# Second attention of a decoder trunk: heads in pairs of column halves, output projection placed between the head steps

## The chip, the cores and the metric

One core of a Trainium2 chip runs the kernel. The metric is the device time of one execution in microseconds (us), as the median of several runs. TensorE (PE, its weight loads PEld), VectorE (DVE), ScalarE (ACT), GpSimd (POOL) and SyncE (SP, which issues the weight DMAs) each work through their own list of instructions in program order and wait for each other by semaphores.

## The reference

Two layers of a decoder on a batch of 256 tokens, width 1024, all in float32. Layer 0 is sparse attention and a dense SwiGLU. Layer 1, where the change lies, is multi-head latent attention and then a top-2-of-8 expert SwiGLU:

```python
def mla_mixer(h, ...):                      # h: (1, 256, 1024), 16 heads
    cq, ckv, k_pe = _split(h @ w_in, [384, 256, 32])
    q = (rmsnorm(cq, q_a_norm) @ w_uq).reshape(B, S, 16, 96)
    kv = (rmsnorm(ckv, kv_a_norm) @ w_ukv).reshape(B, S, 16, 128)
    k_nope, v = kv[..., :64], kv[..., 64:]
    ...                                     # k_pe joined to every head, QK-norm, rotary on 32 columns
    o = causal_attention_blocks(q, k, v)    # softmax(q k^T / sqrt(96), causal) v
    return o.reshape(B, S, 1024) @ w_out    # w_out: 1024 x 1024
x = x + mla_mixer(rmsnorm(x)); h = rmsnorm(x)
y = sum over e of combine[:, e] * swiglu(h, w_gate[e], w_up[e], w_down[e])   # 8 experts, inner width 3584
```

## The kernel before, in words

**Products.** A large product is made of three matmuls in a rounded format: the data and the weight are each split into a high and a low part, and high x high, low x high and high x low are added in PSUM. The weights come from memory in chunks of at most 128 x 2048 floats, numbered in the order in which they are used (`C_LAT`, `C_HEADS`, `C_OUTO`, `C_ROUTE`, `C_MOE` are the first chunks of the latent projection, the head projections, the output projection, the router and the experts). ACT makes the high part of a chunk, DVE the low part (`split`, lines 487 and 954). `split_to(c)` in the list of ACT or DVE says how far this must have come at that place. A chunk's high slot and raw slot are used again when a later chunk comes round, which is counted by `mm_done`, the number of chunks that PE has finished.

**Group stage.** The 16 heads are projected in four groups of four (chunks `C_HEADS` to `C_HEADS`+7). For each group ACT squares, DVE normalises and rotates (lines 1330 to 1370), PE transposes each head (`turn_group`, line 2001) and ACT copies the transposed heads to `qkT` (`group_evac`, line 748).

**Head stage.** `heads(NH, NH, ...)` stands in the lists of PE, ACT, DVE and POOL and runs over the 16 heads one by one. For each head: PE makes the logits (lines 1797, 1798) in PSUM bank 4 or 5; DVE adds the mask and takes the row maximum (1061, 1071) into one of four buffers `lg1[h % 4]`; ACT takes exponentials and row sums (559, 561); DVE takes the reciprocal (1075) and scales the first 128 columns (1077), POOL scales the other 256 (1664); PE transposes the result (1807) into bank 6 or 7, ACT copies it to `pT1` (554); PE multiplies by V (1815, 1816) into half of the rows of bank 0 or 1; after every second head ACT makes the high part `a_hi` (566) and DVE the low part `a_lo` (1082, semaphore `at_olo`). The heads overlap: PE's list has, for step s, the logits of head s, the transposes of head s-3 and the V product of head s-4.

**Output projection.** After `at_olo` has reached 16 (all pairs of heads), PE multiplies by the four chunks of `w_out` (lines 1696, 1697, 1700), adds nothing in between but one set of transposes, and the router follows (`route`, line 2042, in two halves, each after a residual on DVE, line 1227, and transposes, line 1742). SP loads the first expert chunks: four when raw slots come free, then it waits for `at_olo` = 16 and issues chunks 4, 5, 13, 14, 15, then 6 to 11 as slots come free, and from chunk 16 on it needs the experts' order (semaphore `order_set`), which is made from the router's output.

The first attention of the same kernel (layer 0) already runs in pairs: `pair_step`, `pair_mix`, `head_turn` (lines 1749 to 1788) on PE with `pair_logits`, `pair_norm`, `pair_low` on DVE.

## Time and profile before

| | us |
|---|---|
| median of 3 runs (lowest, highest) | 1339.3 (1339.26, 1339.61) |
| the profiled execution | 1338.47 |
| its span | 1336.3 |
| PE, DVE, ACT, POOL busy | 1276.0, 749.7, 633.7, 39.0 |
| head stage, 417.4 to 451.2 us of the span | 33.8 |
| output projection, 451.2 to 474.1 us | 22.9 |
| experts, from 492.4 us to the end | 844 |

The span is the stretch from the first to the last instruction of the profiled execution. "Busy" of PE counts matmuls whose ends are modelled and overlap, so the distance between two starts is the better measure of what one costs. Groups of rows from the trace stand further below; all their times are microseconds from the start of the span.

### The profile page before, as it was taken

How to read it: one execution, taken by the hardware profiler on the slowest of the kernel's cores; microseconds unless marked ns; L12 is line 12 of the kernel's file. 1: busy time of each engine (PE TensorE's matmuls, PEld its weight loads, DVE VectorE, ACT ScalarE, POOL GpSimd, SP SyncE). 2: the span in 40 equal slices, each digit the busy share in tenths (PEclk: the TensorE clock that was granted, in tenths of full speed). 3: DMA queues.
4: the chain of work that ended last, by engine and by line, in shares of the span. 5: the costliest groups of instructions: out<-in, count | busy, mean ns of one | idle time of the engine just before them, and what ended most of it. 6: DMA issues, size and time to landing. Idle time of an engine off the chain costs nothing.

```text
span 1336.3 us, 15885 instructions
## 1 busy us (share of the span) xinstructions
PE 1276.0 (95%) x6208; PEld 899.4 (67%) x6209; DVE 749.7 (56%) x933; ACT 633.7 (47%) x730; POOL 39.0 (3%) x48
## 2 busy tenths in 40 slices
PE   7987999999987989999999999999999999999997
PEld 6765788888875778475847565766656675838572
DVE  5876465444487458464727464736646543837370
ACT  5575562434358537263626353625444533626350
POOL 1012000000002200000000000000000000000000
PEclk9998999999998979999999999999999999999999
DMA  9632455364353458799999999999999999999996
GB/s 341 222 127 65 155 189 189 116 228 149 103 165 136 189 213 318 305 390 411 421 421 421 421 417 417 421 421 420 421 418 417 420 421 420 421 418 418 420 421 251
DMA packets 88757, 422.92 MB, mean 316 GB/s; under 512 B 8561, under 2 KB 15463, under 8 KB 57959
## 3 DMA queue, kind: packets, MB, share of 16 engines
q1 hardware_dynamic: 87468, 419.10, 79.5%
q0 software_dynamic: 992, 2.69, 0.6%
q8 instruction: 50, 0.82, 0.2%
q14 instruction: 29, 0.23, 0.0%
q10 hardware_dynamic: 218, 0.08, 0.0%
HBM read 420.77 MB, written 1.07 MB: 316 GB/s over the span
## 4 chain that ended last, share of the span: by engine, by line
PE 84%; DVE 7%; DMA 4%; ACT 3%; issue 2%; SPq 0%; DVEq 0%; ACTq 0%
PE PS L2151 12%; PE PS L2127 11%; PE PS L2131 11%; PE PS L2128 11%; PE PS L2143 7%; PE PS L1696 7%; PE PS L1700 7%; PE PS L1697 7%; DMA raw<-in_w_down_o_dram 3%; DVE w_r L954 2%; PE PS L2158 1%; PE PS L2067 1%; PE PS L2076 1%; ACT w_r L487 1%; PE PS L1815 1%
## 5 line engine op out<-in xcount | busy, mean ns | idle before, releaser
L1377 DVE TENSOR_TENSOR w_r<-raw,w_r 128x2048 fp32r<-128x2048 f32 (+1 forms) x150 | 314.8, 2102 | 179.3 <-ACT w_r L784 178.8
L784 ACT ACTIVATE w_r<-raw 128x2048 fp32r<-128x2048 f32 (+1 forms) x150 | 264.9, 1766 | 205.9 <-PE PS L2131 118.6
L2127 PE MATMUL PS<-w_r,a_hi 128*128 128x512 f32 x512 | 201.8, 394 | 0.0
L2128 PE MATMUL PS<-w_r,a_lo 128*128 128x512 f32 x512 | 199.9, 390 | 0.0
L2151 PE MATMUL PS<-raw,xs 128*64 128x512 f32 (+1 forms) x856 | 169.9, 543 | 0.0
L954 DVE TENSOR_TENSOR w_r<-raw,w_r 128x2048 fp32r<-128x2048 f32 (+4 forms) x69 | 139.3, 2044 | 40.2 <-ACT w_r L487 40.0
L1696 PE MATMUL PS<-w_r,a_hi 128*128 128x512 f32 (+4 forms) x384 | 144.4, 380 | 6.0 <-DVE a_lo L983 5.1
L1697 PE MATMUL PS<-w_r,a_lo 128*128 128x512 f32 (+4 forms) x384 | 141.9, 373 | 0.0
L487 ACT ACTIVATE w_r<-raw 128x2048 fp32r<-128x2048 f32 (+4 forms) x69 | 115.2, 1719 | 15.4 <-PE PS L1700 12.6
L2151 PEld LDWEIGHTS PS<-raw,xs 128*64 128x64 f32 x856 | 58.8, 137 | 92.8 <-issue 84.2
L2127 PEld LDWEIGHTS PS<-w_r,a_hi 128*128 128x128 f32 x512 | 96.2, 188 | 28.0 <-issue 8.5
L2131 PE MATMUL PS<-w_r,a_hi 128*128 128x512 f32 x411 | 112.3, 390 | 0.9 <-DVE w_r L1377 0.9
L2128 PEld LDWEIGHTS PS<-w_r,a_lo 128*128 128x128 f32 x512 | 96.2, 188 | 19.8
L1700 PE MATMUL PS<-w_r,a_hi 128*128 128x512 f32 (+4 forms) x384 | 97.7, 374 | 0.3 <-DVE w_r L954 0.3
L1377 DVE TENSOR_TENSOR slots_r<-slots,w_r 128x2048 fp32r<-128x2048 f32 (+1 forms) x30 | 62.8, 2095 | 57.9 <-ACT w_r L784 57.8
L2131 PEld LDWEIGHTS PS<-w_r,a_hi 128*128 128x128 f32 x411 | 77.0, 188 | 17.8 <-DVE w_r L1377 1.8
L1696 PEld LDWEIGHTS PS<-w_r,a_hi 128*128 128x128 f32 x384 | 72.8, 189 | 20.6 <-issue 7.7
L2143 PE MATMUL PS<-raw,es 128*64 128x512 f32 x376 | 83.1, 593 | 0.0
L1697 PEld LDWEIGHTS PS<-w_r,a_lo 128*128 128x128 f32 x384 | 72.9, 190 | 11.3
L1700 PEld LDWEIGHTS PS<-w_r,a_hi 128*128 128x128 f32 x384 | 69.5, 190 | 13.5 <-DVE w_r L954 1.7
L784 ACT ACTIVATE w_r<-slots 128x2048 fp32r<-128x2048 f32 (+1 forms) x30 | 53.0, 1767 | 48.1 <-DMA slots<-in_w_gate_o_dram 23.8
L2127 PE MATMUL PS<-w_r,e_hi 128*128 128x512 f32 x160 | 64.1, 400 | 1.7 <-ACT w_r L784 1.7
(318 smaller groups left out, 1445.9 us busy)
## 6 DMA issues: line engine op xcount, KB each, us to landing
raw<-in_w_down_o_dram SPq DMA_DIRECT2D x94, 1024.0 KB, 18.8
raw<-in_w_gate_o_dram SPq DMA_DIRECT2D x53, 1024.0 KB, 14.6
raw<-in_w_up_o_dram SPq DMA_DIRECT2D x51, 1024.0 KB, 15.1
raw<-in_w_gate_o_dram SPq DMA_DIRECT2D x53, 768.0 KB, 12.1
raw<-in_w_up_o_dram SPq DMA_DIRECT2D x53, 768.0 KB, 11.7
slots<-in_w_down_o_dram SPq DMA_DIRECT2D x18, 1024.0 KB, 18.3
raw<-in_w_in_e_dram SPq DMA_DIRECT2D x12, 1024.0 KB, 10.5
raw<-in_w_down_e_dram SPq DMA_DIRECT2D x11, 1024.0 KB, 4.8
```

The source lines that it names most:

```text
L487: nc.scalar.activation(w_r[:, hi_slot(c), 0:n], raw[:, c % RAW, 0:n], ACT.Copy).then_inc(hi_done, 1)
L784: nc.scalar.activation(w_r[:, high_slot(g), 0:w], place_of(n)[:, 0:w], ACT.Copy).then_inc(hi_done, 1)
L954: nc.vector.tensor_tensor(w_r[:, c % RAW, 0:n], raw[:, c % RAW, 0:n], w_r[:, hi_slot(c), 0:n], ALU.subtract).then_inc(lo_done, 1)
L1377: nc.vector.tensor_tensor(place_r(n)[:, 0:w], place_of(n)[:, 0:w], w_r[:, high_slot(g), 0:w], ALU.subtract).then_inc(lo_done, 1)
L1696: nc.tensor.matmul(dst, xh, wh, start=first, stop=False)
L1697: nc.tensor.matmul(dst, xl, wh, start=False, stop=False)
L1700: return nc.tensor.matmul(dst, xh, wl, start=False, stop=last)
L2127: nc.tensor.matmul(PS[:, bank, :], xh(x), hi[:, c0:c0 + NT], start=first, stop=False)
L2128: nc.tensor.matmul(PS[:, bank, :], xl(x), hi[:, c0:c0 + NT], start=False, stop=False)
L2131: ins = nc.tensor.matmul(PS[:, bank, :], xh(x), lo[:, c0:c0 + NT], start=False, stop=last)
L2143: ins = nc.tensor.matmul(PS[HALF * h:HALF * h + HALF, SMALL_DOWN, :], es[:, f, :], w[:, kk * D + h * NT:kk * D + (h + 1) * NT], start=f == ...
L2151: ins = nc.tensor.matmul(PS[HALF * h:HALF * h + HALF, bank + b, 0:n], xs[:, at, :], w[:, c0:c0 + n], start=at == 0, stop=at == DC - 1)
```

## The change

Heads of the second attention go in pairs, with the semaphores and functions of the first attention: a step s has the logits of pair s, the transposes of pair s-2 and the V product of pair s-3. All transposes use bank 6, all V products bank 7, where the two heads of a pair use the two column halves of the array. The matmuls of the output projection are cut into 16 pieces (`out_piece(n, dc)`: column half n, rows of 128 inputs dc, six matmuls each) that stand in PE's list between the logits and the second transposes of a step. Steps 0 and 1 stand inside the end of the group stage. On ACT and DVE the splits of chunks stand earlier or elsewhere, and the last pair's result stands behind the first expert chunk's split. SP has chunks 4, 5, 6 before its wait for `at_olo`, and POOL does four heads before it issues one DMA.

```diff
-        lg1, z1 = place(z0, "lg1", [P, 4, LOG])
+        lg1, z1 = place(z0 + 2 * TT * GH * ROPE, "lg1", [P, 4, LOG])
...
# SP
+            sp.wait_ge(sem("at_qk"), 2 * NH)
+            for n in (4, 5):
+                expert_chunk(0, n, 0)
+            ring_chunk(6)
             sp.wait_ge(sem("at_olo"), NH)
-            for n in (4, 5, 13, 14, 15):
+            for n in (13, 14, 15):
                 expert_chunk(0, n, 0)
-            for n in range(6, 12):
+            for n in range(7, 12):
                 ring_chunk(n)
# ACT (heads() is removed)
+            def late_step(s):
+                if s >= 3:
+                    pair_out(s, NH)               # a_hi of pair s-3 from bank 7
+                for r in range(2):
+                    if 2 <= s < NH // 2 + 2:
+                        probs_turned(NH + 2 * s - 4 + r)   # waits at_tr; copy to pT1
+                    if s < NH // 2:
+                        head_exp(NH + 2 * s + r)  # waits at_max
...
-                split_to(C_HEADS + 2 * g + 4)
+                if g == 0:
+                    split_to(C_HEADS + 6)
+                elif g == 1:
+                    split_to(C_HEADS + 7)
+                elif g == 2:
+                    split_to(C_OUTO + 1)
                 if g >= 1:
                     group_evac(g - 1, 0)
-                split_to(C_HEADS + 2 * g + 5)
+                if g < 2:
+                    split_to(C_HEADS + 7 + g)
             group_evac(GROUPS - 2, 1)
+            late_step(0)
             group_evac(GROUPS - 1, 0)
+            late_step(1)
             group_evac(GROUPS - 1, 1)
-            heads(NH, NH, lg1, pT1)
-            spare_root(3)
+            split_to(C_OUTO + 2)
+            late_step(2)
+            late_step(3)
+            split_to(C_OUTO + 3)
+            late_step(4)
+            split_to(C_OUTO + 4)
+            for s in range(5, NH // 2 + 2):
+                late_step(s)
             split_to(C_MOE)
             esplit(0)
+            late_step(NH // 2 + 2)
+            spare_root(3)
             esplit(1)
# DVE, in the last group, before its reciprocal
+                if g == GROUPS - 1:
+                    pair_logits(0, NH)
...
-                split_to(C_HEADS + 2 * g + 4)
+                if g < 3:
+                    split_to(C_HEADS + 6 + g)
...
-                split_to(C_HEADS + 2 * g + 5)
-            heads(NH, NH, lg1, False)
+                if g == 2:
+                    split_to(C_OUTO + 1)
+            pair_logits(1, NH)
+            pair_norm(0, NH)
+            split_to(C_OUTO + 2)
+            pair_logits(2, NH)
+            pair_norm(1, NH)
+            pair_logits(3, NH)
+            pair_norm(2, NH)
+            pair_low(0, NH)
+            split_to(C_OUTO + 3)
+            pair_logits(4, NH)
+            pair_norm(3, NH)
+            pair_low(1, NH)
+            split_to(C_OUTO + 4)
+            for s in range(5, NH // 2):
+                pair_logits(s, NH)
+                pair_norm(s - 1, NH)
+                pair_low(s - 3, NH)
+            pair_norm(NH // 2 - 1, NH)
+            pair_low(NH // 2 - 3, NH)
+            split_to(C_MOE)
+            pair_low(NH // 2 - 2, NH)
-            split_to(C_MOE)
             esplit(0)
+            pair_low(NH // 2 - 1, NH)
             dve.wait_ge(mm_done, C_OUTO + 2)
             residual(0, PS[:, 0:2, :])
# POOL
+            heads(NH, 4, lg1)
             pool.wait_ge(sem("grp_tr"), NH)
             pool.dma_start(ffg[:, :], ffn_norm_o.to_broadcast([P, D])).then_inc(sem("ffg_in"), 16)
-            heads(NH, NH, lg1)
+            heads(NH + 4, NH - 4, lg1)
# PE (heads() is removed; pair_mix and head_turn serve both attentions)
+            def out_piece(n, dc):
+                c = C_OUTO + 2 * n + dc // 4
+                if dc % 4 == 0:
+                    pe.wait_ge(hi_done, c + 1)
+                    pe.wait_ge(lo_done, c + 1)
+                pe.wait_ge(sem("at_olo"), NH // 2 + dc + 1)
+                ...
+                for t in range(TT):
+                    high(PS[:, 2 * n + t, :], xh, xl, hi[:, dc % 4, :], dc == 0)
+                    ins = low(PS[:, 2 * n + t, :], xh, lo[:, dc % 4, :], dc == DC - 1)
+            def late_step(s):
+                if s >= 3:
+                    pair_mix(s - 3, NH)           # waits at_pt of the pair, at_olo of the pair before
+                if 2 <= s < NH // 2 + 2:
+                    head_turn(NH + 2 * s - 4)
+                if s < NH // 2:
+                    pe.wait_ge(sem("at_add"), NH + 2 * s)
+                    pe.wait_ge(sem("grp_ev"), 2 * (2 * s + 2))
+                    ...                           # logits of the two heads
+                if s >= 4:
+                    ins = out_piece(0, s - 4)
+                    if s - 4 == 3:
+                        ins.then_inc(mm_done, 1)
+                if s >= 5:
+                    out_piece(1, s - 5)
+                if 2 <= s < NH // 2 + 2:
+                    head_turn(NH + 2 * s - 3)
...
+            late_step(0)                          # after the last head projection and its transposes
             turn_group(GROUPS - 2, 1)
             turn_group(GROUPS - 1, 0)
+            late_step(1)
             turn_group(GROUPS - 1, 1)
+            pe.wait_ge(sem("grp_ev"), 2 * NH)
+            late_step(2)
+            late_step(3)
...
-            project(C_OUTO, 2, 4, NT, 0)
-            part(C_OUTO + 2, True, False, 0, 4, NT, 2)
+            for s in range(4, NH // 2 + 3):
+                late_step(s)
+            out_piece(0, DC - 1).then_inc(mm_done, 1)
+            out_piece(1, DC - 2).then_inc(mm_done, 1)
             norm_turn(3, 0)
-            part(C_OUTO + 3, False, True, 4, 4, NT, 2)
+            out_piece(1, DC - 1).then_inc(mm_done, 1)
```

## Rows read from the trace of the kernel before

**Rows 1.** Windows view: length; PE, PEld, DVE, ACT, POOL busy; clock; DMA share; GB/s
```profile
417.40:451.20 33.80, 31.95 (x176) 21.72 (x176) 21.52 (x120) 26.82 (x90) 16.23 (x16) 1.00 0.05 16
451.20:474.10 22.90, 22.84 (x105) 18.97 (x106) 7.77 (x6) 10.31 (x11) 0.00 (x0) 1.00 0.91 367
...
560.00:1336.00 776.00, 762.46 (x3652) 489.62 (x3648) 417.69 (x298) 345.61 (x263) 0.00 (x0) 1.00 1.00 411
```

**Rows 2.** Waits of the DMA queue: total us, times, longest
```profile
SPq L400 <- DVE a_lo L1082: 47.2, 1, 47.2
...
SPq L403 <- DVE order L1454: 14.3, 1, 14.3
```

**Rows 3.** Timeline of one head: start us, us, engine, line, operation [idle before]
```profile
429.84 0.40 ACT L559 ACTIVATE lg<-lg,nm 128x128 f32<-128x128 f32 x1
...
429.97 0.49 PE L1797 MATMUL PS<-qkT 96*128 96x128 f32 x2
...
430.73 0.36 ACT L566 ACTIVATE a_hi<-PS 128x256 fp32r<-128x256 f32 x1
430.73 0.49 PE L1807 MATMUL PS<-cst,lg 128*128 128x128 f32 x3
430.93 0.29 DVE L1061 CUSTOM_DVE_ANT_0 lg<-PS,cst 128x128 f32<-128x128 f32 x1 [0.74 <-PE PS L1798]
...
431.16 0.65 PE L1815 MATMUL PS<-pT,v 128*64 128x256 f32 x2
...
431.61 0.17 DVE L1071 TENSOR_SCALAR nm<-nm 128x2 f32<-128x2 f32 x1
...
431.95 0.38 PE L1797 MATMUL PS<-qkT 96*128 96x128 f32 x1
```

**Rows 4.** Timeline, a pair step of the first attention
```profile
105.93 0.41 DVE L1045 TENSOR_TENSOR mix_lo<-PS,mix_hi 128x256 fp32r<-128x256 f32 x1
...
106.48 0.65 PE L1756 MATMUL PS<-pT,v 128*64 128x256 f32 x4 [1.65 <-DVE mix_lo L1045]
...
107.29 0.55 PE L1768 MATMUL PS<-cst,lg 128*128 128x128 f32 x3
```

**Rows 5.** Timeline, same attention: a wait for a low part, DVE after logits
```profile
120.82 0.80 PE L1696 MATMUL PS<-w_r,mix_hi 128*128 128x512 f32 x1 [3.67 <-DVE mix_lo L1045]
...
131.35 0.17 DVE L1030 TENSOR_SCALAR nm<-nm 128x2 f32<-128x2 f32 x1
...
132.25 0.41 DVE L1045 TENSOR_TENSOR a_lo<-PS,a_hi 128x256 fp32r<-128x256 f32 x1
```

**Rows 6.** Timeline, same attention: transposes, copy, next V product
```profile
141.74 0.52 PE L1768 MATMUL PS<-cst,lg 128*128 128x128 f32 x3 [0.67 <-ACT pT L536]
142.30 0.49 ACT L536 ACTIVATE pT<-PS 128x384 f32<-128x384 f32 x1 [0.70 <-PE PS L1768]
142.84 0.65 PE L1756 MATMUL PS<-pT,v 128*64 128x256 f32 x4 [0.58 <-ACT pT L536]
```

**Rows 7.** Timeline, end of the group stage
```profile
408.54 2.28 DVE L954 TENSOR_TENSOR w_r<-raw,w_r 128x2048 fp32r<-128x2048 f32 x1
...
409.55 1.92 ACT L487 ACTIVATE w_r<-raw 128x2048 fp32r<-128x2048 f32 x1
...
417.43 0.46 PE L1797 MATMUL PS<-qkT 96*128 96x128 f32 x2 [1.12 <-ACT qkT L748]
```

**Rows 8.** Windows view around falls of the granted clock
```profile
119.60:126.40 6.80, 5.58 (x14) 3.97 (x16) 3.38 (x7) 2.79 (x5) 1.92 (x2) 0.51 0.00 0
366.60:368.80 2.20, 0.19 (x2) 0.18 (x2) 1.27 (x3) 2.20 (x11) 0.00 (x0) 1.00 0.56 179
368.80:372.20 3.40, 3.40 (x12) 3.40 (x13) 1.52 (x6) 0.30 (x3) 0.00 (x0) 0.51 0.17 62
373.80:375.90 2.10, 0.26 (x4) 0.03 (x1) 0.88 (x2) 1.83 (x4) 0.00 (x0) 1.00 0.50 138
```

**Rows 9.** Timeline, second half of the router
```profile
477.73 3.21 PE L2042 MATMUL PS<-cst,xT 128*128 128x8 f32 x16 [0.88 <-DVE xT L1382]
```

More of the change, by code:

```diff
@@ L522, in spare_root, with pair_out, probs_turned @@
                 nc.scalar.activation(nst[:, q, 12:13], nst[:, q, 12:13], ACT.Sqrt)
+            def pair_out(s, h0=0):
+                p = s - 3
+                act.wait_ge(sem("at_pv"), h0 + 2 * p + 2)
+                nc.scalar.activation(mix_hi[:, p, :] if p < 4 and not h0 else a_hi[:, p, :], PS[:, 7, 0:S], ACT.Copy)\
+                    .then_inc(sem("at_ohi"), 1)
+            def probs_turned(h):
+                act.wait_ge(sem("at_tr"), h + 1)
+                if h >= 2:
+                    act.wait_ge(sem("at_pv"), h - 1)
+                nc.scalar.activation((pT if h < NH else pT1)[:, h % 2, :], PS[:, 6, 0:LOG], ACT.Copy).then_inc(sem("at_pt"), 1)
@@ L1006, in token_scale, with pair_logits @@
                 return r.to_broadcast(shape)
-            def pair_logits(s):
-                for h in (2 * s, 2 * s + 1):
+            def pair_logits(s, h0=0):
+                logits = lg1 if h0 else lg
+                for h in (h0 + 2 * s, h0 + 2 * s + 1):
                     dve.wait_ge(sem("at_qk"), h + 1)
@@ L1030, in pair_logits, with pair_norm @@
                     nc.vector.tensor_scalar(nm[:, h, 0:2], nm[:, h, 2:4], -1.0, None, ALU.mult).then_inc(sem("at_max"), 1)
-            def pair_norm(s):
-                for h in (2 * s, 2 * s + 1):
+            def pair_norm(s, h0=0):
+                logits = lg1 if h0 else lg
+                for h in (h0 + 2 * s, h0 + 2 * s + 1):
                     dve.wait_ge(sem("at_exp"), 2 * h + 2)
@@ L1037, in pair_norm, with pair_low @@
                     dve.wait_ge(sem("at_rcp"), h + 1)
-                    nc.vector.tensor_scalar(lg[:, h % 4, 0:P], lg[:, h % 4, 0:P], rs[:, h, 2:3], None, ALU.mult)\
+                    nc.vector.tensor_scalar(logits[:, h % 4, 0:P], logits[:, h % 4, 0:P], rs[:, h, 2:3], None, ALU.mult)\
                         .then_inc(sem("at_norm0"), 1)
-            def pair_low(p):
-                dve.wait_ge(sem("at_ohi"), p + 1)
-                high, low = (mix_hi, mix_lo) if p < 4 else (a_hi, a_lo)
+            def pair_low(p, h0=0):
+                dve.wait_ge(sem("at_ohi"), h0 // 2 + p + 1)
+                high, low = (mix_hi, mix_lo) if p < 4 and not h0 else (a_hi, a_lo)
@@ L1766, in head_turn @@
                     pe.wait_ge(sem("at_pt"), h)
+                logits = lg if h < NH else lg1
                 for k in range(3):
[L1768 removed]
+                    ins = nc.tensor.transpose(PS[:, 6, k * P:(k + 1) * P], logits[:, h % 4, k * P:(k + 1) * P], ident)
                 ins.then_inc(sem("at_tr"), 1)
```

176 lines of the change are left out of this document (49 added, 127 removed).

## The prediction

> **What bounds the kernel now.** I read the windows by stage first, then the waits of the DMA queue, then the timeline around the second attention. From 560 us to the end the DMA engines are busy all the time at 411 GB/s and PE nearly so [rows 1]: both are full, and no time is to be had there. This stage cannot start early: from chunk 16 on SP needs the experts' order, for which it waited 14.3 us with all its slots served [rows 2], and the order comes from the router, behind the attention. So whatever the second attention and its output projection gain or lose up to the router moves everything behind it by the same amount. The term to be found is the start of the router's second half, 477.73 us [rows 9], counted from the start of the head stage, 417.43 us [rows 7]: 60.3 us now.
>
> In the head stage PE is the bound. It is busy 31.95 of 33.8 us [rows 1], and one head goes by in 1.98 us (429.97 to 431.95) with no wait of PE marked: 0.76 us logits, 0.43 transposes, 0.79 V product [rows 3]. The output projection behind it is dense too, 22.84 of 22.9 us; less one set of transposes (0.8) that is 22.1 us, or 1.38 us for each of 16 pieces, at the full clock [rows 1]. Two heads and two pieces now cost 3.96 + 2.76 = 6.72 us.
>
> **What PE saves.** Two V products in column halves run at the same time: in the first attention the pair takes 0.81 us (106.48 to 107.29) [rows 4], where two single ones take 1.58 [rows 3]. That is 0.77 us a pair, 6.2 us for eight. Steps 0 and 1 move two pairs of logits (3.0 us) into the group stage, where PE waits anyway. So 9.2 us of PE work leave the path. If PE stayed the bound, this would be the gain.
>
> **What the new order makes wait.** It does not stay the bound, because there is now one bank for transposes, one for V products, and four logits buffers for two pairs. The chain, from the start of a step's second transposes (of head 2s-3):
> - 0.56 us until another engine sees them (141.74 to 142.30) [rows 6]. Only now is the buffer free for the logits of head 2s+1, for which DVE has waited, and everything behind it in DVE's list waits too: `pair_norm(s-1)` and `pair_low(s-3)`.
> - 0.68 us mask and maximum (430.93 to 431.61) [rows 3], 0.90 us to the start of the low part behind two scalings (131.35 to 132.25) [rows 5], 0.55 us until PE goes on behind the low part (105.93 to 106.48) [rows 4]. Sum 2.69 us.
> - Then the next V product, which needs bank 7 empty: 0.81; first transposes 0.43 to 0.47; two heads' logits 1.52; the pieces; and the second transposes again.
>
> A step with logits so takes 2.69 + 0.81 + 0.45 + 1.52 = 5.5 us without pieces, 6.85 with one, 8.2 with two, against 6.72 now for two heads and two pieces. The pieces stand between the logits and the second transposes, so they lengthen this chain instead of filling the 2.2 us in which PE waits for the low part. The first attention shows such waits: 1.65 us [rows 4] and 3.67 us [rows 5] for a low part.
>
> **The sum from the start of step 2 to the router's second half.**
> - Steps 2 and 3: 9.3 us. ACT first splits a weight chunk (1.9) [rows 7], so the second transposes start only at 2.45 (1.9 + 0.49 + 0.06). DVE's split ends at 4.2 (1.95 + 2.28), its first logits at 5.1, ACT's exponentials at 6.0 (0.89, 429.84 to 430.73) [rows 3], the copy behind them at 6.55; then 0.81, 0.45, 1.52 to the second transposes of step 3.
> - Step 4: 6.75. Step 5: 8.6 (the chain, and 0.4 more because DVE's split of a chunk ends late). Steps 6 and 7: 8.15 each, 16.3.
> - Step 8, no logits: 2.69 + 0.81 + 0.45 + 2.76 = 6.6 (rounded down for an overlap of the last transposes). Step 9: DVE has no logits to wait for, and the copy alone decides, 1.10 us (141.74 to 142.84) [rows 6]: 1.10 + 0.81 + 0.45 + 2.76 = 5.1.
> - The end: after the last copy ACT splits the first expert chunk (1.92), DVE its low part (2.28) [rows 7], and only then comes the last pair's low part, 5.8 us behind the last transposes; piece 1.38, residual 1.4, transposes 0.8, last piece 1.38: 10.8. Then ACT's list holds the router back (a copy 0.6, squares 1.25, a split 1.92, squares 1.25, a copy 0.6, from the residual on): 4.1.
>
> Sum 9.3 + 6.75 + 8.6 + 16.3 + 6.6 + 5.1 + 10.8 + 4.1 = 67.55, against 60.3: **7.25 us more**. The bounds of this term: the 2.69 us could be 0.3 smaller or larger in each of seven steps, plus or minus 2.
>
> **The group stage and the forward splits.** PE and DVE are about equally loaded there, so the splits that DVE loses in groups 0 and 1 (placed earlier, beside the latent projections) give nothing. In group 3 DVE loses one split of 2.28 [rows 7] and gains two heads' logits (1.5): 0.8 earlier. Against that the last heads' copies on ACT now stand behind four heads' exponentials, of which the last two need logits that PE makes after the third transposes. I get 417.7 in place of 417.43 at the full clock and 419.5 at half. I take +0.6, bounds -1 and +2. POOL's norms and the DMA of `ffg` trade places: the issue is half a us, its data are needed 50 us later, nothing. The moved buffer: nothing.
>
> **SP's order.** Chunks 4, 5, 6 are issued some 6 to 20 us earlier; 13, 14, 15 wait for the last low part, at about 475.8 instead of 451.2. Then nine chunks of 1 MB at 2.5 us each (1 MB over 411 GB/s [rows 1]) take until 498.5, and the order comes at about 496.6 + 8 = 504. Hidden, by some 6 us; if that cover were gone, a late chunk would cost what it is late, 2.5 us each.
>
> **The clock.** Where PE waits, its granted clock may fall from 2.4 to 1.2 GHz. After the wait of 3.67 us [rows 5] it was at half for 6.8 us; after one of 2.0 us (366.6 to 368.8) it fell to half for 3.4 us; after one of 1.8 us (373.8 to 375.9) it did not fall [rows 8]. The change has one wait of 3.65 us (step 3) and six of 2.2 to 2.7. A stretch of 3.4 us at half does 1.7 us less. If the first costs 2 us, as PE is only part of that chain, and two of six fall, 3.4: +5.4, from which I take 0.4 off because the order in which PE finds work at 404 to 409 us improves. So **+5**, bounds 0 and +13.
>
> **Forecast.** 0.6 + 7.25 + 5 = 12.85 us. The profiled execution took 1338.5, 2.2 outside its span, and is 0.8 below the median of 1339.3; the sum is made against its own time, 1351.3, and put on the median 1352.1. I predict **1352**.
>
> The Trainium skill, page TensorEngine Tiling (Array Packing), has two rules that pull apart here. Under Theoretical Speedup it gives up to 2x for a dimension of at most 64; the pair of 0.81 against 1.58 agrees [rows 3, 4]. By that rule alone the change would be 6.2 us faster, 1333. Under Performance Considerations, PSUM Bottleneck, it says that packing does not speed up the evacuation of PSUM, which may become the bound; the waits for a low part agree [rows 4, 5], and that rule gives the loss.
>
> **Rivals.**
> - *Same chain, no fall of the clock.* 0.6 + 7.25: 1347. For it: after 1.65 and 1.8 us of waiting the clock stayed. Against it: the row of 2.0 us, and many waits. 0.22.
> - *The clock falls in nearly every step.* Eight stretches at half, 1.7 each, and a second behind the 3.65 us: 15; 0.6 + 7.25 + 15: 1362. For it: every step repeats the wait. Against it: long dense pieces in each step. 0.10. The Trainium skill describes such a pattern, page TensorE: Matmul & The Clock Gate, section on psum-queue depth-cycling: small idles between groups of matmuls make the clock go up and down; this case's first attention shows single falls only.
> - *PE stays the bound: faster.* If DVE sees the second transposes early enough, or the lists shift so that the low part is done before PE wants the bank, the waits vanish: PE's own work is 6 x 1.52 + 16 x 0.45 + 8 x 0.81 + 16 x 1.38 = 44.9, and some 7 us of transposes, residual and router follow: 52 against 60.3, 1331. It decides where PE's wait in a step falls below 1.2 us (7.25 us over seven steps is 1.0 each). For it: the saved V products are certain. Against it: a buffer that cannot be free earlier. 0.13.
> - *Gain and loss cancel,* at a wait near 1.2 us: 1339.5, 0.07.
> - *The steps do not do what they say:* the last pair hidden behind the expert split makes PE wait much longer, or the order comes after late chunks; 1356 or more, inside the range. 0.03.
>
> **How the numbers follow.** The forecast has 0.45, its own range 1348 to 1357. Slower is 0.45 + 0.22 + 0.10 + 0.03 = 0.80, faster 0.13 plus 0.01 for a mishap of the sum, 0.14, within 0.2% 0.06. (0.2%, 2.7 us, is about what a measurement of this kernel tells from no change.) The range leaves out the faster rival and the extreme of the clock: 1341 to 1360.
>
> **What would show it.** In the changed trace: V products of pairs that wait about 2.2 us for `a_lo` in steps 4 to 8 (steps 6 and 7 8.1 us apart); a wait of 3.6 us for `pT` in step 3; one of about 1.2 us before the second last pieces; stretches at half clock between 420 and 475 us; the router's second half at 485 to 491 us; the DMA stage as before, later by the same amount. Wrong would be: PE with no waits in the pair steps (then faster), SP's wait for the order gone (then DMA decides), or a router that starts late with an experts' stage that is shorter.

## The result

The changed kernel takes 1353.05 us (median of four executions, 1350.31 to 1355.11), against 1339.28 us before (1336.88 to 1339.61): 13.8 us, ratio 1.0103, 95% interval 1.0086 to 1.0119. It is slower. The profiled execution took 1350.31 us, 11.8 more than the profiled one of before.

The windows view of the kernel before and of the changed one, from the start of the head stage (step 2) to the router's second half:

```profile
417.43:477.73 60.30, 57.55 (x304) 43.20 (x305) 32.53 (x131) 38.92 (x105) 16.23 (x16) 1.00 0.41 161
```
```profile
416.60:491.36 74.76, 57.33 (x288) 44.43 (x289) 33.04 (x109) 37.92 (x90) 13.89 (x15) 0.84 0.24 92
560.00:1336.00 776.00, 770.12 (x3690) 492.93 (x3691) 418.25 (x301) 347.66 (x267) 0.00 (x0) 1.00 1.01 416
```

The stretch is 74.76 us long in place of 60.30. PE is busy for as long in it (57.33 us, before 57.55), with less work, since a part of it now runs at the half clock. So PE idles 17.4 us instead of 2.8. The mean granted clock is 0.84, before 1.00. The DMA stage from 560 us on is as it was [rows 1].

The rest of the difference is small. The group stage is read from the first transposes of its latents to the start of step 2:

```profile
365.80 0.82 PE L1985 MATMUL PS<-cst,latn 128*128 128x128 f32 x6
```
```profile
365.02 0.82 PE L2009 MATMUL PS<-cst,latn 128*128 128x128 f32 x6
...
416.60 0.55 PE L1783 MATMUL PS<-cst,lg 128*128 128x128 f32 x3 [1.69 <-ACT qkT L752]
```

417.43 - 365.80 = 51.63 us before [rows 7], 51.58 after. The 0.8 us by which step 2 starts earlier were there ahead of this stage, in code that the change leaves alone; e1, e2 and e3 below also have 51.6 us here, with latents between 364.9 and 368.0 us, e5 to e7 51.0 to 52.5. Behind the router's second half there are 858.6 us before and 856.7 after. So the spans differ by -0.8 - 0.05 + 14.5 - 1.8 = 11.8 us. The first and the last of these are within what differs from one profiled execution to the next: over the thirteen traces of this document the latents start between 364.9 and 369.9 us, and from the router's second half to the end it is 856.5 to 859.1 us, in no order that follows the changes. The medians, which average over this, are 13.8 us apart.

One full step (step 5 to 6) of the changed kernel, all of it at the full clock, in the timeline of PE and DVE:

```profile
447.34 0.49 PE L1783 MATMUL PS<-cst,lg 128*128 128x128 f32 x3
...
447.97 0.29 DVE L1042 CUSTOM_DVE_ANT_0 lg<-PS,cst 128x128 f32<-128x128 f32 x1 [4.32 <-PE PS L1783]
...
448.65 0.17 DVE L1052 TENSOR_SCALAR nm<-nm 128x2 f32<-128x2 f32 x1
...
449.55 0.41 DVE L1068 TENSOR_TENSOR a_lo<-PS,a_hi 128x256 fp32r<-128x256 f32 x1
...
450.10 0.65 PE L1770 MATMUL PS<-pT,v 128*64 128x256 f32 x4 [2.27 <-DVE a_lo L1068]
...
450.90 0.55 PE L1783 MATMUL PS<-cst,lg 128*128 128x128 f32 x3
451.29 0.39 PE L1831 MATMUL PS<-qkT 96*128 96x128 f32 x2
...
452.41 0.58 PE L1708 MATMUL PS<-w_r,a_hi 128*128 128x512 f32 x1
...
455.35 0.49 PE L1783 MATMUL PS<-cst,lg 128*128 128x128 f32 x3
```

This is the chain of the prediction, link by link: second transposes 447.34, DVE's logits 0.63 later (it had idled for them), maximum 0.68, low part 0.90 later, V product 0.55 later: 2.76 us (forecast 2.69). Then 0.80 for the V products, 0.39 transposes, 1.12 logits, 2.94 for two pieces. The step is 8.01 us. The logits are faster than [rows 3] gave (1.12 for two heads, not 1.52), each piece slower (1.47, not 1.38).

The end of the stage:

```profile
477.65 1.90 ACT L802 ACTIVATE w_r<-raw 128x2048 fp32r<-128x2048 f32 x1
479.45 0.38 ACT L532 ACTIVATE a_hi<-PS 128x256 fp32r<-128x256 f32 x1
...
479.58 2.29 DVE L1388 TENSOR_TENSOR w_r<-raw,w_r 128x2048 fp32r<-128x2048 f32 x1 [5.00 <-ACT w_r L802]
481.79 0.42 DVE L1068 TENSOR_TENSOR a_lo<-PS,a_hi 128x256 fp32r<-128x256 f32 x1
...
482.26 0.50 PE L1708 MATMUL PS<-w_r,a_hi 128*128 128x512 f32 x1 [0.60 <-DVE a_lo L1068]
...
491.36 1.92 PE L2070 MATMUL PS<-cst,xT 128*128 128x8 f32 x16 [0.88 <-ACT xT L807]
```

The last pair's `a_hi` waits behind ACT's expert split and its `a_lo` behind DVE's; PE has other pieces meanwhile and waits 0.60 us.

The stretches at the half clock are what the trace adds to the chain. Between 416.6 and 491.4 us there are four with a granted clock of 0.50 (418.2 to 428.5, 431.9 to 435.3, 438.7 to 445.5, 459.2 to 462.6), 23.9 us together; before there was none in this stretch.

### The profile page after: what moved, and what is told of

The parts are those of the page before. It is cut to its first block, busy times and chain, and to the rows that moved or that the text cites. A ratio compares the mean times of both kernels' runs of the same rounds, so it can differ in the third digit from the quotient of the medians.

```text
span 1348.1 us, 15897 instructions
## 1 busy us (share of the span) xinstructions
PE 1274.8 (95%) x6208; PEld 900.8 (67%) x6209; DVE 749.2 (56%) x933; ACT 634.1 (47%) x730; POOL 38.1 (3%) x48
## 3 DMA queue, kind: packets, MB, share of 16 engines
q0 software_dynamic: 992, 2.69, 0.6%
## 4 chain that ended last, share of the span: by engine, by line
PE 84%; DVE 7%; ACT 3%; DMA 3%; issue 2%; SPq 0%; DVEq 0%; ACTq 0%
PE PS L2179 13%; PE PS L2155 11%; PE PS L2159 11%; PE PS L2156 11%; PE PS L1708 7%; PE PS L2171 7%; PE PS L1709 7%; PE PS L1712 7%; DMA raw<-in_w_down_o_dram 2%; PE PS L2186 1%; DVE w_r L974 1%; PE PS L2095 1%; PE PS L2104 1%; PE PS L1783 1%; ACT w_r L491 1%
## 5 line engine op out<-in xcount | busy, mean ns | idle before, releaser
L1708 PE MATMUL PS<-w_r,a_hi 128*128 128x512 f32 (+4 forms) x384 | 147.0, 387 | 6.8 <-DVE a_lo L1003 6.2
L1712 PE MATMUL PS<-w_r,a_hi 128*128 128x512 f32 (+4 forms) x384 | 101.9, 375 | 0.0
L1712 PEld LDWEIGHTS PS<-w_r,a_hi 128*128 128x128 f32 x384 | 69.9, 191 | 13.6 <-DVE w_r L974 1.4
## 6 DMA issues: line engine op xcount, KB each, us to landing
raw<-in_w_in_e_dram SPq DMA_DIRECT2D x12, 1024.0 KB, 10.3
```

Source lines behind the costliest of these rows:

```text
L1708: nc.tensor.matmul(dst, xh, wh, start=first, stop=False)
L1712: return nc.tensor.matmul(dst, xh, wl, start=False, stop=last)
```

## The experiments

All of them are read on the same stretch, from the start of step 2 to the router's second half, since what lies ahead of it varies by up to 5 us from one profiled execution to the next. Stretch and half are those of the one profiled execution, which need not be a typical one: it is 2.7 us below the median for the changed kernel, 3.4 us for e3 and 7 us for e6. "Half" is the time in it at the half clock: the sum of twice (1 - granted clock) times the length, over windows of 1 us. Medians are over all executions of a kernel, ratios over those of the kernel before on the same chip (its medians: 1339.45 us for e1 to e4, 1338.38 for e5 to e8, 1339.23 for e9 to e11). The changed kernel has its median from a group of its own (1339.28 for the kernel before), so a difference from it is good to about 1 us.

| kernel | stretch, us | half, us | median, us | ratio (95%) |
|---|---|---|---|---|
| before | 60.30 | 0 | 1339.3 | 1 |
| changed | 74.76 | 23.9 | 1353.05 | 1.0103 (1.0086-1.0119) |
| e1 pieces last | 62.44 | 13.6 | 1342.4 | 1.0024 (1.0013-1.0035) |
| e2 low part first | 66.26 | 13.7 | 1346.5 | 1.0049 (1.0032-1.0065) |
| e3 filler | 68.11 | 6.8 | 1347.3 | 1.0059 (1.0042-1.0075) |
| e4 SP's order | 74.78 | 23.9 | 1353.2 | 1.0099 (1.0082-1.0116) |
| e5 both orders | 63.07 | 13.7 | 1343.1 | 1.0033 (1.0021-1.0045) |
| e6 and a filler | 61.34 | 3.4 | 1345.1 | 1.0051 (1.0037-1.0064) |
| e7 order of the halves | 73.26 | 20.6 | 1352.5 | 1.0111 (1.0095-1.0127) |
| e8 pieces at the end | 81.34 | 37.5 | 1361.1 | 1.0163 (1.0147-1.0178) |
| e9 both, queues cleared | 58.26 | 13.7 | 1337.7 | 0.9984 (0.9973-0.9994) |
| e10 e9 and a filler | 57.77 | 6.8 | 1336.4 | 0.9974 (0.9963-0.9984) |
| e11 halves in turn | 82.47 | 27.2 | 1359.5 | 1.0144 (1.0125-1.0163) |

Executions of one and the same kernel differ by several us, and they are ordered by the mean granted clock of the whole execution. Of the 49 executions of the kernel before in the three groups, the 11 with a clock of 0.987 or 0.988 took 1336.3 to 1338.0 us, the 7 with 0.982 took 1340.4 to 1342.4 us. By the means (0.9875 and 1336.9 us, 0.982 and 1341.6 us) that is an estimate of 0.3 us for each us more at the half clock.

**e1: the pieces behind the second transposes.**

```diff
+                if 2 <= s < NH // 2 + 2:
+                    head_turn(NH + 2 * s - 3)
                 if s >= 4:
                     ins = out_piece(0, s - 4)
...
                     out_piece(1, s - 5)
-                if 2 <= s < NH // 2 + 2:
-                    head_turn(NH + 2 * s - 3)
```

> The changed kernel with the pieces of the output projection moved, on TensorE alone, from in front of the second transposes of a step to behind them. Theory (the way back of a logits buffer sets the step: second transposes, logits of the odd head, scalings, low part, next product with the values, and the pieces lengthen that way): the pieces now run while VectorE works, the 2.27 us waits for the low part nearly go, a full step falls from 8.01 us to about 5.7 us, the head stage shortens by 10 to 12 us, and the half-clock spans inside it (24 us between 418 and 463 us) shrink: 1337 to 1343 us. Rival 1 (the pieces cost what they cost wherever they stand, the step is TensorE's own work): within 2 us of the changed kernel. Rival 2 (the loss is in the clock alone, by the waits' number and not by the order): the steps shorten only by the waits' 2.3 us each, the clock stays as it was: about 1346 us.

Measured: 1342.4 us, 10.7 us faster than the changed kernel, within the theory's band. V products of pairs, in PE's timeline:

```profile
453.30 0.65 PE L1770 MATMUL PS<-pT,v 128*64 128x256 f32 x4
...
458.98 0.65 PE L1770 MATMUL PS<-pT,v 128*64 128x256 f32 x4
```

They are 5.68 us apart and wait for nothing (the two before them still wait 0.80 and 1.12 us for a low part). The same pieces that lengthen the chain in front of the transposes fill DVE's time behind them. Both rivals fall: the time is in the order, and it is more than the waits. A part of it is the clock's, since 10.3 us less are at the half clock.

**e2: the low part ahead of the logits.**

```diff
-            pair_logits(3, NH)
             pair_norm(2, NH)
             pair_low(0, NH)
+            pair_logits(3, NH)
             split_to(C_OUTO + 3)
-            pair_logits(4, NH)
             pair_norm(3, NH)
             pair_low(1, NH)
+            pair_logits(4, NH)
             split_to(C_OUTO + 4)
             for s in range(5, NH // 2):
-                pair_logits(s, NH)
                 pair_norm(s - 1, NH)
                 pair_low(s - 3, NH)
+                pair_logits(s, NH)
```

> The changed kernel with one order changed on VectorE: in the steps from 3 on the scalings of the previous pair and the low part of the pair before stand ahead of the logits of the step's pair instead of behind them. Theory: the low part no longer waits for the second transposes, so the wait of the product with the values falls from 2.27 us to the order of 0.5 us or none; what is left of the way through the logits buffer (logits, exponentials, scalings of the odd head) now has a whole step of slack; about 1.7 us in each of five steps goes, 8 to 9 us, 1344 us, and 1340 us if the clock comes back with it. Rival (the buffer of the logits itself binds, not the queue behind it): the wait only moves to the transposes (for the scalings), 1351 to 1353 us.

Measured: 1346.5 us, 6.6 us faster than the changed kernel. From the fifth V products on the wait is 0.58 us, for the copy of the transposes. It brought less than forecast because one wait grew (ACT, DVE and PE timeline):

```profile
432.45 1.90 ACT L491 ACTIVATE w_r<-raw 128x2048 fp32r<-128x2048 f32 x1
...
434.38 2.29 DVE L974 TENSOR_TENSOR w_r<-raw,w_r 128x2048 fp32r<-128x2048 f32 x1 [2.85 <-ACT w_r L491]
...
436.58 0.16 DVE L1059 RECIPROCAL rs<-rs 128x2 f32<-128x2 f32 x1
...
440.23 0.70 PE L1770 MATMUL PS<-pT,v 128*64 128x256 f32 x4 [4.54 <-ACT pT L540]
```

ACT's weight split runs from 432.45, DVE waits for it and splits from 434.38, and only at 436.58 do the scalings start that had been ready. The logits come behind them, an exponential on ACT waits for the logits until 438.81, and the copy of the odd head's transposes, ready since 435.7, stands behind it (439.71): the V products wait 4.54 us. The theory of the chain stands; a second queue shows behind it.

**e3: PE kept at work, the chain untouched.**

```diff
+                if 2 <= s < NH // 2:
+                    pe.wait_ge(sem("at_add"), NH + 2 * s + 1)
+                    for _ in range(4):
+                        nc.tensor.matmul(PS[:, 4, 0:S], ident, cst[:, 0:S], start=True, stop=True)
```

> The changed kernel with four added f32 matmuls of 128x256, whose result nobody reads, behind the second transposes of steps 2 to 7: TensorE works in the stretch in which it waited for the low part, and the chain through VectorE is as before. The added work is about 1.7 us a step at full clock, within the wait of 2.27 us. Theory (the waits let the clock fall, and the half clock costs about 5 us of the 14): the granted clock stays at 1.00 from 418 to 463 us, and the kernel is 4 to 6 us faster in spite of more work, 1348 us. Rival 1 (the clock costs nothing, since the chain runs on the other engines): within 1 us of the changed kernel. Rival 2 (the falls come from something else than the waits, such as the f32 transposes): the half-clock spans stay, and the added work at half clock, 3.5 us in a wait of 2.3, makes it 3 to 6 us slower.

Measured: 1347.3 us, 5.7 us faster than the changed kernel with more work. Windows of the changed kernel and of this one:

```profile
428.00:438.00 10.00, 6.48 (x31) 4.88 (x29) 5.92 (x23) 6.05 (x16) 1.99 (x3) 0.81 0.00 0
438.00:448.00 10.00, 8.79 (x34) 6.82 (x34) 3.89 (x11) 4.57 (x12) 1.82 (x2) 0.66 0.01 2
458.00:468.00 10.00, 7.61 (x36) 6.19 (x38) 3.00 (x17) 3.33 (x11) 2.23 (x4) 0.83 0.48 174
```
```profile
428.00:438.00 10.00, 8.98 (x54) 6.79 (x53) 6.72 (x26) 7.52 (x22) 3.81 (x4) 1.00 0.01 2
438.00:448.00 10.00, 9.45 (x56) 7.83 (x55) 5.71 (x21) 4.90 (x15) 1.91 (x2) 1.00 0.00 1
458.00:468.00 10.00, 8.87 (x54) 6.75 (x54) 3.81 (x17) 3.72 (x10) 3.81 (x4) 1.00 0.67 281
```

The clock is 1.00 where it was 0.81, 0.66 and 0.83. Only the first stretch at half (418 to 425 us) is left. 17.1 us less at half make the stretch 6.65 us shorter. The mean clock of whole executions says the same of all four: 0.984 to 0.988, where the changed kernel has 0.978 to 0.980. So the waits cost time in themselves, and once more because the clock falls at them. Both rivals, a clock that costs nothing and falls that come from something else than the waits, fail.

The 6.65 us are a net sum, for in step 2 the filler itself ran at the half clock (0.50 from 418.8 to 424.87 us) and stood in the way of the first V products of a pair. The changed kernel, then this one, in PE's timeline:

```profile
422.87 1.12 PE L1770 MATMUL PS<-pT,v 128*64 128x256 f32 x4 [3.13 <-ACT pT L540]
...
427.60 0.85 PE L1783 MATMUL PS<-cst,lg 128*128 128x128 f32 x3
```
```profile
421.16 3.78 PE L1845 MATMUL PS<-cst 128*128 128x256 f32 x8 [1.54 <-DVE nm L1042]
...
424.87 0.65 PE L1770 MATMUL PS<-pT,v 128*64 128x256 f32 x4
...
427.37 0.49 PE L1783 MATMUL PS<-cst,lg 128*128 128x128 f32 x3
```

From the start of step 2 (416.60 and 416.48) the V products come after 6.27 us in the changed kernel and after 8.39 us here, 2.1 us later. From them to the second transposes of step 3 it is 4.73 us there, at the half clock, and 2.50 us here, at the full clock: 2.2 us. So in these two steps the filler gave back the half clock's cost and took as much. From second transposes to second transposes the changed kernel takes 2.0 us more than this one in step 4, 2.9 in step 5, 1.7 in step 7, and the same in the others. With the 2.2 us that makes an estimate of 8.8 us for what the 23.9 us at the half clock cost the changed kernel, 0.37 us for each. The Trainium skill, page TensorE: Matmul & The Clock Gate, section on psum-queue depth-cycling, says that frequent small idles between groups of matmuls make the clock swing; the falls of the changed kernel, which this kernel with its shorter idles lacks, agree.

**e4: SP's order as before.**

```diff
-            sp.wait_ge(sem("at_qk"), 2 * NH)
-            for n in (4, 5):
-                expert_chunk(0, n, 0)
-            ring_chunk(6)
             sp.wait_ge(sem("at_olo"), NH)
-            for n in (13, 14, 15):
+            for n in (4, 5, 13, 14, 15):
                 expert_chunk(0, n, 0)
-            for n in range(7, 12):
+            for n in range(6, 12):
                 ring_chunk(n)
```

> The changed kernel with the order of the weight loads on SP as it was before the change (all of 4, 5, 13 to 15 and the rest behind the wait for the last low part). Theory: these loads are covered by the loads that fill the queues until the end of the kernel, so it costs nothing, within 1 us of the changed kernel. Rival (the memory stream bounds the end of the kernel, and loads brought forward by 20 us are a gain that hides part of the loss): 2 to 5 us slower than the changed kernel.

Measured: 1353.2 against 1353.05 us, the stretch 74.78 against 74.76. Nothing, as the theory had it.

**e5: e1 and e2 together**, and two splits moved (shown against e1 and e2 together, DVE's list; on ACT the fourth split stands behind `late_step(5)` instead of `late_step(4)`).

```diff
-            split_to(C_OUTO + 3)
             pair_norm(3, NH)
             pair_low(1, NH)
+            split_to(C_OUTO + 3)
             pair_logits(4, NH)
-            split_to(C_OUTO + 4)
...
                 pair_low(s - 3, NH)
+                if s == 6:
+                    split_to(C_OUTO + 4)
                 pair_logits(s, NH)
```

> The changed kernel with the two reorderings together (the pieces behind the second transposes on TensorE; scalings and low part ahead of the logits on VectorE), and with two weight splits moved: the third split of the output projection's weights stands on VectorE behind the low part of its step instead of in front of the scalings, the fourth comes two steps later on both engines. Theory: from step 4 on TensorE waits for nothing but the copy of the transposes, full steps take 5.7 us, and the 4.5 us stall that the split caused when the low part was put first is gone; the heads up to the router's second half take 58 to 60 us instead of 74.8: 1338 to 1341 us, level with the kernel before. Rival 1 (the pieces' order alone gives all there is): as with the pieces moved alone, 1342.4 us. Rival 2 (the pairs in column halves, 0.77 us saved each, come out in full once nothing waits): 1333 to 1335 us, faster than before.

Measured: 1343.1, no better than e1 alone. The forecast missed. Full steps are 5.7 us as said, but the early ones are not; e6 has the same order, and shows why.

**e6: e5, the filler of e3 in steps 2 and 3 only, the expert split behind the last pair** (ACT's list; DVE's likewise).

```diff
-            esplit(0)
             late_step(NH // 2 + 2)
+            esplit(0)
```

> As the kernel with both reorderings, with two things more: the first expert split stands behind the last pair's copy and low part again, on ScalarE and VectorE, as before the change; and in steps 2 and 3, which have no pieces yet, four added f32 matmuls of 128x256 that nobody reads keep TensorE at work in its longest waits. Theory: the half-clock spans in the first half of the heads go (2 to 4 us), the wait in front of the second-last pieces goes (0.6 us): 1.5 to 4 us faster than with both reorderings alone, 1335 to 1338 us, and that beats the kernel before by some 0.2%. Rival (the early steps are bound by the chain through the other engines at any clock): within 1 us of it.

Measured: 1345.1, a miss too. Its profiled execution was its fastest, 1338.2, with a mean clock of 0.988; the other four took 1343 to 1347, with clocks of 0.980 to 0.982. So in most executions the filler did not keep the clock up, and where it fell in them no trace shows. Its trace names the wait that was left (DVE, ACT and PE timeline):

```profile
433.31 2.28 DVE L975 TENSOR_TENSOR w_r<-raw,w_r 128x2048 fp32r<-128x2048 f32 x1
...
436.18 0.17 DVE L1053 TENSOR_SCALAR nm<-nm 128x2 f32<-128x2 f32 x1
...
436.38 0.40 ACT L546 ACTIVATE lg<-lg,nm 128x128 f32<-128x128 f32 x1 [3.07 <-DVE nm L1053]
...
437.28 0.47 ACT L540 ACTIVATE pT<-PS 128x384 f32<-128x384 f32 x1
...
437.80 0.65 PE L1772 MATMUL PS<-pT,v 128*64 128x256 f32 x4 [2.44 <-ACT pT L540]
```

DVE's split (2.28 us) delays the logits, ACT's exponential waits for them, the copy of the odd head's transposes (long ready) is queued behind that exponential, and the V products wait 2.44 us for the copy. e5's trace has the same wait of 2.44 us.

**e7: the odd head's products behind both of the even head's.**

```diff
-                for r in range(2):
-                    nc.tensor.matmul(dst[r], v[r][:, 0, :], probs[:, r, 0:S], start=True, stop=False)
-                for r in range(2):
-                    nc.tensor.matmul(dst[r][:, P:S], v[r][:, 1, :], probs[:, r, S:LOG], start=False, stop=True)\
-                        .then_inc(sem("at_pv"), 1)
+                for rs_ in ([0], [1]) if h0 else ([0, 1],):
+                    for r in rs_:
+                        nc.tensor.matmul(dst[r], v[r][:, 0, :], probs[:, r, 0:S], start=True, stop=False)
+                    for r in rs_:
+                        nc.tensor.matmul(dst[r][:, P:S], v[r][:, 1, :], probs[:, r, S:LOG], start=False, stop=True)\
+                            .then_inc(sem("at_pv"), 1)
```

> The changed kernel with one order changed in the products with the values of the second attention: both products of the even head and then both of the odd head, so that the two column halves never follow each other directly. The arithmetic is the same. Theory (the two halves run beside each other only when their instructions alternate, 0.80 us a pair against 1.57 us, and the product is a link of the chain that sets the step): about 0.7 us more a pair at full clock, 5 to 7 us slower than the changed kernel, 1359 us. Rival 1 (the saving is hidden, since TensorE waits anyway): within 1 us of it. Rival 2 (the halves do not run beside each other at all, 0.80 us is only the shorter instruction): within 1 us too, and the pair's length in the trace stays at 0.80 us.

Measured: 1352.5; the pair's products still take 0.81 us (447.94 to 448.75). The theory's premise fails: the edit did not make the two halves run one after the other, so it says nothing on their worth; e11 does. Rival 2 (no overlap at all) also expected 0.80 us; against it stand the 1.58 us that the same four products take for two single heads [rows 3], and e11.

**e8: no pieces between the steps.**

```diff
-                if s >= 4:
-                    ins = out_piece(0, s - 4)
...
-                if s >= 5:
-                    out_piece(1, s - 5)
...
+            for dc in range(DC):
+                ins = out_piece(0, dc)
...
+            for dc in range(DC - 1):
+                ins = out_piece(1, dc)
```

> The changed kernel with the placement of the output projection undone: none of its pieces between the steps, all sixteen behind the last pair (the order of the pieces and their signals otherwise as in the changed kernel). Theory (a step without pieces takes about 5.2 us by the chain, and each piece costs 1.46 us of TensorE wherever it stands; in between the steps a piece costs its own length, because it stands on the chain): the same time as the changed kernel within 3 us, most likely 1 to 3 us slower at equal clock, 1350 to 1357 us. Rival (it is the placing of the pieces that made the kernel slower): 8 us or more faster, near 1340 us.

Measured: 1361.1 us, 8.1 us slower than the changed kernel; the theory's sign, and beyond its band. The rival, that placing the pieces between the steps is the harm, is refuted: pieces in front of the second transposes are better than no pieces between the steps. Windows of the steps and of what follows:

```profile
421.50:471.70 50.20, 32.85 (x154) 23.83 (x154) 24.25 (x99) 26.19 (x74) 13.89 (x15) 0.69 0.15 53
471.70:502.80 31.10, 29.60 (x136) 23.79 (x137) 8.74 (x10) 10.91 (x16) 0.00 (x0) 0.90 0.59 225
```

Without pieces PE is busy 65% of the steps, the clock is 0.69, and a step takes 6.9 us where 5.2 was expected at the full clock. The stretch is 6.6 us longer, with 13.6 us more at the half clock; at the 0.37 us of e3 that is an estimate of 5 us. So the pieces cost the chain their length, and what they gave back is most likely the clock; no run has this order with the clock kept up.

**e9: e5 with the queues cleared.** Both copies of transposes stand ahead of the exponentials on ACT, the weight splits behind the logits on DVE, the expert split behind the last pair.

```diff
                 for r in range(2):
                     if 2 <= s < NH // 2 + 2:
                         probs_turned(NH + 2 * s - 4 + r)
+                for r in range(2):
                     if s < NH // 2:
                         head_exp(NH + 2 * s + r)
```

> As the kernel with both reorderings, without any filler, and with what its trace still shows as a wait taken away: on ScalarE both copies of the transposes stand ahead of the exponentials (the copy of the odd head was queued behind the exponential of the next even head, and that one behind a weight split on VectorE; the product with the values waited 2.4 us for it), the third and fourth split stand behind the logits of their step on VectorE, and the first expert split behind the last pair's low part on both engines as before the change. Theory: one wait of 2.4 us and one of 0.6 us go, steps from 4 on are TensorE's own 5.7 us; from the start of step 2 to the router's second half 58 to 60 us, the kernel before has 60.3: level with or up to 2 us faster than the kernel before at the same granted clock, 1337 to 1341 us. Rival (what TensorE gains in the steps it pays back as half clock in the first three steps, whatever stands on the other engines): as with both reorderings alone, 1343 us.

Measured: 1337.7 us, 0.16% faster than the kernel before (interval 0.06 to 0.27%, less than the 0.2% that the prediction took as the least to be told from no change), 15.4 us faster than the changed one; the stretch is 58.26 us. The windows of the whole stretch and of steps 5 to 9:

```profile
420.57:478.83 58.26, 52.60 (x288) 39.67 (x289) 33.54 (x109) 36.87 (x90) 13.88 (x15) 0.88 0.34 131
438.26:466.08 27.82, 26.34 (x156) 19.73 (x155) 13.99 (x53) 14.74 (x45) 7.68 (x8) 1.00 0.29 115
```

**e10: e9 with the filler of e3 in steps 2 and 3 only, `range(2)` in place of `range(4)`.**

> As the kernel before it in this call, with two added f32 matmuls of 128x256 that nobody reads in steps 2 and 3, half of what the earlier kernel with a filler had. Theory of the clock (half clock between 420 and 432 us comes from the idle TensorE of steps 2 and 3, and costs 2 to 4 us): 1 to 3 us faster than the same kernel without them, 1335 to 1339 us. Rival (whether the clock falls there is drawn anew in each execution, and the filler only adds work): within 1 us of it, with the same spread of several us between executions.

Measured: 1336.4, 0.26% faster than the kernel before (0.16 to 0.37%). Against e9 it is 1.2 us, and the intervals overlap; half clock in the stretch is 6.8 us in place of 13.7. The mean clock of whole executions points the same way (median 0.985, e9 0.982). So what the filler in steps 2 and 3 is worth is not settled; it is small.

**e11: the halves forced one behind the other** by a wait of PE for the even head's end.

```diff
                 for r in range(2):
+                    if h0 and r:
+                        pe.wait_ge(sem("at_pv"), h + 1)
                     nc.tensor.matmul(dst[r], v[r][:, 0, :], probs[:, r, 0:S], start=True, stop=False)
-                for r in range(2):
                     nc.tensor.matmul(dst[r][:, P:S], v[r][:, 1, :], probs[:, r, S:LOG], start=False, stop=True)\
                         .then_inc(sem("at_pv"), 1)
```

> The changed kernel with the two column halves of the second attention forced one behind the other: TensorE waits for the end of the even head's product with the values before it starts the odd head's. With the order alone changed, the pair still took 0.81 us. Theory (the halves run beside each other by themselves, 0.80 us a pair, and the product is a link of the chain that sets the step): a pair takes 1.5 to 1.7 us, and since TensorE's waits don't cover a link of the chain, each of the eight steps is 0.7 to 0.9 us longer: 6 to 8 us slower than the changed kernel, 1359 to 1361 us. Rival (the product runs beside the wait for something else, so its length is hidden): within 1.5 us of the changed kernel.

Measured: 1359.5, 6.4 us slower than the changed kernel. Two pairs in PE's timeline:

```profile
443.51 0.62 PE L1772 MATMUL PS<-pT,v 128*64 128x256 f32 x2 [2.28 <-DVE a_lo L1068]
443.97 0.38 PE L1773 MATMUL PS<-pT,v 128*64 128x128 f32 x2
444.41 0.65 PE L1772 MATMUL PS<-pT,v 128*64 128x256 f32 x2
444.89 0.48 PE L1773 MATMUL PS<-pT,v 128*64 128x128 f32 x2
445.30 0.90 PE L1784 MATMUL PS<-cst,lg 128*128 128x128 f32 x3
...
482.42 0.65 PE L1772 MATMUL PS<-pT,v 128*64 128x256 f32 x2 [0.58 <-ACT pT L540]
...
484.13 0.55 PE L1784 MATMUL PS<-cst,lg 128*128 128x128 f32 x3
```

The first pair takes 1.79 us, its last 0.3 us at the half clock; the second, all at the full clock, takes 1.71 us, against 0.80: 0.91 more, the signal included. Eight times that is 7.3 us. The stretch is 7.7 us longer, with 3.3 us more of it at the half clock, so the two parts can't be told apart to the last us; but the extra time of the products is not hidden, as the rival had it. The Trainium skill, page TensorEngine Tiling (Array Packing), section Theoretical Speedup, gives up to 2x; 1.58 us for two single heads [rows 3] to 0.80 us for the pair agrees.

## Why the prediction came out

- **Forecast 1352, measured 1353.05; the likeliest case.** The mechanism is the one named: e1 and e2 break the chain at two places and take away 10.7 and 6.6 of the 13.8 us. That the number came out within 1 us is in part luck. The chain was taken 1.6 us too long and the group stage 0.65 us, the clock 3.8 us too cheap, and these partly cancel (see below).
- **The sum without the clock, 67.55 us: about 66.0.** Steps 2 and 3 at the full clock would be 8.8 us (forecast 9.3). The rest is read in e3, which has the changed kernel's chain without the other falls, from second transposes to second transposes: step 4 6.66 (forecast 6.75), step 5 8.22 (8.6), steps 6 and 7 8.01 each (8.15), step 8 6.70 (6.6), step 9 5.01 (5.1), the end 14.61 (14.9). Each is within 0.4; the logits taken too dear and the pieces too cheap nearly cancel.
- **Steps 2 and 3.** They took 11.0 us. The V products came 6.27 us after the start of step 2 (forecast 6.55, of which the wait is 3.13, forecast 3.65); behind them come 4.73 us at the half clock, 2.50 at the full one in e3. The cost of the half clock here, 2.2 us, is near the 2 us that the prediction took for its first stretch, but it began with step 2 itself (418.2 us) and not behind step 3's wait.
- **The clock, +5: too little, 8.8 us.** It is inside the bounds. The prediction took two of six later waits to be followed by 3.4 us at half each, 1.7 us a time. There were three such stretches, one of them 6.8 us long, and they cost 2.0, 2.9 and 1.7 us. Of the five waits of 2.3 us three have a fall within 1.3 us of the start of the V products behind them (430.73, 439.03, 458.11), two (450.10, 467.80) have none.
- **The group stage, +0.6 us: wrong.** It is -0.05 us. The exponentials put ahead of the last copies, and the split taken from group 3, left no trace; PE's wait for `qkT` at step 2 is 1.69 us where it was 1.12.
- **SP's order, 0.** Right (e4). Chunks 13 to 15 went out at 482.2, not 475.8, and the wait for the order is 14.6 us, before 14.3 [rows 2].
- **Column halves, 0.77 us a pair.** Right in size (0.80 us the pair). That their length counts, since the products lie on the chain, is shown by e11: without the overlap the changed kernel would have been slower still. With the chain broken on both engines and the queues cleared (e9) the whole change gains 1.6 us, of 9.2 us of PE work taken off the path.
- **The evacuation of PSUM, named as what gives the loss.** Only in part: the low part itself takes 0.41 us. It came late since it stood behind the logits in DVE's list, and with the order turned round (e2) PE's wait for it went from 2.27 to 0.58 us, for a copy. More buffers for the logits, which would cut the same chain, were not tried.
- **PE's waits:** 2.27 or 2.28 us for `a_lo` in steps 4 to 8, forecast 2.2. Before the second last pieces 0.60, forecast 1.2.
- **"PE stays the bound" (1331)** did not happen, and e9 shows its limit: with nothing but PE in steps 5 to 9 the stretch is 58.26 us, not 52. All of the 13.7 us at half lie in its first 17.7 us (420.57 to 438.26, clock 0.61). Another part is likely the start itself: pieces begin with step 4, and until then PE has nothing to fill the latency of the first pairs. No run separates the two.
- **The other signs.** The router's second half came at 491.36 us, just behind the 485 to 491 that were named; steps 6 and 7 are 8.01 us apart, named 8.1.
- **What stays open:** why the clock falls at some waits of 2.3 us and not at others, and where it fell in e6's other executions.

## What to carry to other kernels

Before work is put into the gaps of a pipelined loop, find the transfer of ownership (here the second transposes, which free a buffer) that the slowest engine waits for: work put ahead of it lengthens the loop, the same work behind it fills the wait (here steps of 8.0 us became steps of 5.7). Then look at each in-order queue for an early item waiting behind a late one, and clear those together, since each shows only once the one in front is gone. Here a tensor engine that waited 2.3 us in every round paid again in its clock, an estimated 8.8 of 14.5 us. A filler of unread products can show this, but it must end before the work that it stands in front of is ready: in step 2 it ran at the half clock and took back what it gave.

## What had not been expected of the hardware

The two column halves overlap even when the odd head's instructions stand behind both of the even head's (e7). The records of e7 for the first product of both heads:

```profile
L1771 PE MATMUL PS<-pT,v x2: 401/416/430, 447.9 to 448.0; 128*64 128x256 f32 x2
```

A product is two records. In e11 those of one head start 0.3 us apart (443.5 and 443.8); here two start within 0.1 us, so they seem to belong to the two heads. The even head's second product, which stands between them in the program, starts only at 448.4. This much is read from two records; the pair's 0.81 us, against 1.58 for two single heads [rows 3], does not hang on it. So the instructions of the two halves need not alternate to overlap; only a wait (e11) kept them apart.

Adding PE work made a kernel faster (e3, 5.7 us), and moving PE work out of the steps made it slower (e8, 8.1 us).
